# First norm: shift and scale of three tiles summed by TensorE; other orders of splits, exponentials and output blocks in the attentions

## The reference, cut to what matters

```python
mod = (jax.nn.silu(c) @ ada_w[l] + ada_b[l]).reshape(B, 3, 3, 1, D)
n = _modulate(_rmsnorm(h, norm_g[l, 0]), mod[:, 0, 0], mod[:, 0, 1])   # n = norm * (1 + scale) + shift
h = h + 0.5 * mod[:, 0, 2] * _swiglu(n, ffn_w_in[l, 0], ffn_w_out[l, 0])
```

## Time and profile before

| | |
|---|---|
| median of three runs | 3486.48 us |
| profiled execution / its span | 3488.39 / 3486.6 us |
| TensorE busy | 3430.1 us, 98% |
| VectorE busy | 2168.9 us, 62% |
| ScalarE busy | 1322.5 us, 38% |
| GpSimd busy | 296.9 us, 9% |
| mean granted clock of TensorE | 0.997 |

### The profile page before, as it was taken

One profiled execution on the slowest core, in us unless ns is written; L12 is line 12 of the kernel. 1 busy time (PEld: TensorE's weight loads), 2 busy tenths in 40 slices (PEclk: granted clock), 3 DMA queues, 4 the chain that ended last, 5 costly groups with the idle time before them and its releaser, 6 DMA issues.

```text
span 3486.6 us, 46915 instructions
## 1 busy us (share of the span) xinstructions
PE 3430.1 (98%) x18494; PEld 2864.6 (82%) x18494; DVE 2168.9 (62%) x3570; ACT 1322.5 (38%) x1950; POOL 296.9 (9%) x376
## 2 busy tenths in 40 slices
PE   9999999999999999999999999999999999999998
PEld 7888966898888988895789888899988897588888
DVE  7555665656554655566576777788776557655444
ACT  4222463333222422246333523355533236643222
POOL 0000231001000100023100000012100001210000
PEclk9999999999999999999999999999999999999999
DMA  7444302434443344330243344344444312013221
GB/s 277 187 157 163 106 24 100 160 130 172 155 160 148 139 163 159 146 112 3 106 160 137 148 163 154 145 151 176 175 169 163 117 67 90 1 49 112 94 97 49
DMA packets 85561, 452.01 MB, mean 130 GB/s; under 512 B 10304, under 2 KB 12544, under 8 KB 48608
## 3 DMA queue, kind: packets, MB, share of 16 engines
q1 hardware_dynamic: 83168, 439.10, 33.8%
q0 software_dynamic: 2176, 9.92, 0.8%
HBM read 446.88 MB, written 2.10 MB: 129 GB/s over the span
## 4 chain that ended last, share of the span: by engine, by line
PE 89%; DVE 5%; ACT 3%; issue 1%; DMA 0%; POOL 0%; DVEq 0%; SPq 0%; ACTq 0%; POOLq 0%
PE ps L658 22%; PE ps L660 22%; PE ps L659 22%; PE ps L2766 2%; PE ps L2767 2%; PE ps L2768 2%; PE ps L3464 1%; ACT P L1852 1%; PE ps L1035 1%; PE ps L1037 1%; PE ps L1036 1%; PE ps L1772 1%; PE ps L1295 1%; PE ps L1297 1%; PE ps L1296 1%
## 5 line engine op out<-in xcount | busy, mean ns | idle before, releaser
L658 PE MATMUL ps<-nH,WH 128*128 128x512 f32 x2256 | 884.2, 392 | 0.4 <-ACT rot L3195 0.4
L660 PE MATMUL ps<-nH,WL 128*128 128x512 f32 x2256 | 884.2, 392 | 0.0
L659 PE MATMUL ps<-nL,WH 128*128 128x512 f32 x2256 | 883.7, 392 | 0.0
L564 DVE TENSOR_TENSOR WL<-raw,WH 128x2048 fp32r<-128x2048 f32 (+2 forms) x297 | 651.1, 2197 | 370.3 <-ACT WH L553 369.2
L553 ACT ACTIVATE WH<-raw 128x2048 fp32r<-128x2048 f32 (+2 forms) x299 | 543.6, 1823 | 573.5 <-PE ps L660 497.2
L658 PEld LDWEIGHTS ps<-nH,WH 128*128 128x128 f32 x2256 | 423.8, 188 | 95.8 <-issue 3.3
L659 PEld LDWEIGHTS ps<-nL,WH 128*128 128x128 f32 x2256 | 423.8, 188 | 93.0 <-issue 0.2
L660 PEld LDWEIGHTS ps<-nH,WL 128*128 128x128 f32 x2256 | 423.8, 188 | 91.5
L624 DVE SCALAR_TENSOR_TENSOR araw<-araw,cB 128x1024 f32<-128x1024 f32 x224 | 275.6, 1230 | 201.5 <-DMA araw<-in_ast 201.1
L658 PE MATMUL ps<-hH,WH 128*128 128x512 f32 x944 | 372.3, 394 | 1.0 <-DVE h L1262 1.0
L660 PE MATMUL ps<-hH,WL 128*128 128x512 f32 x944 | 371.2, 393 | 0.0
(11 more groups left out here) (451 smaller groups left out, 5910.3 us busy)
## 6 DMA issues: line engine op xcount, KB each, us to landing
raw<-in_wst SPq DMA_DIRECT2D x273, 1024.0 KB, 4.8
araw<-in_ast SPq DMA_DIRECT2D x225, 512.0 KB, 5.7
raw<-in_wst SPq DMA_DIRECT2D x18, 512.0 KB, 3.3
araw<-in_wst SPq DMA_DIRECT2D x9, 1024.0 KB, 4.9
row<-in_ast SPq DMA_DIRECT2D x15, 512.0 KB, 10.6
cw<-in_cw POOLq DMA_DIRECT2D x4, 1024.0 KB, 5.9
h<-in_xT SPq DMA_DIRECT2D x4, 512.0 KB, 5.5
raw<-in_wst SPq DMA_DIRECT2D x8, 256.0 KB, 2.7
```

The lines of the kernel that those rows point to most:

```text
L564: dve.q.tensor_tensor(M.WL[k % NW][:, 0:n], M.raw[raw_use[k]][:, 0:n], M.WH[k % NW][:, 0:n].bitcast(F32), ALU.subtract).then_inc(*v_wlo.up(k))
L658: pe.q.matmul(to, hi[:, i, cc], xh, start=i == 0, stop=False)
L659: pe.q.matmul(to, hi[:, i, cc], xl, start=False, stop=False)
L660: t = pe.q.matmul(to, lo[:, i, cc], xh, start=False, stop=i == nk - 1)
```

## The change

- Shift and scale of tiles 0, 1 and 2 (six rows) are no longer summed by VectorE. The host lays these six 1024x128 matrices with the summed index on the partitions, and `rows(f)` on TensorE does 16 one-column fp32 matmuls for tile f (8 for the shift, 8 for the scale) against silu(c) as a column of 8. `rows(0)` stands ahead of rstd, `rows(1)` and `rows(2)` behind it.
- The fillers of 5 and 14 around rstd are gone, the later one is 8 instead of 14; `part` goes in another order; each engine's work at the start is reordered, and SyncE loads the six matrices first, and the broadcast c behind them.
- Attention 1: ScalarE does the copy between the two exponentials of a step, and VectorE does the lone unit's maximum between the two inverses.
- Attention 2: the split of two weight slots moves from ahead of the units to units 10 and 14 (ScalarE), 11 and 15 (VectorE); a small exponential stands ahead of the units; a fifth output block is begun, behind the last unit.

```diff
--- before.py
+++ after.py
@@ -19,7 +19,7 @@
...
@@ -1402,10 +1414,6 @@
                 t = pe.q.matmul(banks[6][:, j:j + 1], lat.scr[2][:, j * 128:j * 128 + 128], M.ones[:, 0:1], start=True,
                                 stop=True)
             t.then_inc(*mm.up(g, "sum"))
-            warm_up(pe, 5, g, "warm1")
-            pe.wait_ge(*v_dg.to(g))
-            pe.q.matmul(banks[7][:, :], M.ones[:, :], lat.scr[3][:, :], start=True, stop=True).then_inc(*mm.up(g, "rstd"))
-            warm_up(pe, 14, g, "warm2")
             ks = [slot_pe_later("ffn_w_in") for _ in range(3)]
             names = [(g, x, 0, f) for x, f in (("a", 0), ("a", 1), ("b", 0), ("b", 1), ("a", 2), ("a", 3))]
             to = []
@@ -1413,6 +1421,26 @@
                 b, free = take(*name)
                 pe.wait_ge(*free)
                 to.append(b)
+            first_bank[:] = [to[4], to[5], to[4]]
+
+            def rows(f):
+
+                pe.wait_ge(*a_cB.to("first"))
+                if f == 2:
+                    pe.wait_ge(*v_mod.to(g, 0))
+                for m in range(2):
+                    pe.wait_ge(*ld_of(8 * m + f))
+                    w = row_tile(8 * m + f)
+                    for i in range(KT):
+                        t = pe.q.matmul(first_bank[f][:, m:m + 1], w[:, 128 * i:128 * i + 128], M.half[:, i:i + 1],
+                                        start=i == 0, stop=i == KT - 1)
+                t.then_inc(*mm.up(g, "row", f))
+
+            rows(0)
+            pe.wait_ge(*v_dg.to(g))
+            pe.q.matmul(banks[7][:, :], M.ones[:, :], lat.scr[3][:, :], start=True, stop=True).then_inc(*mm.up(g, "rstd"))
+            rows(1)
+            rows(2)
 
             def part(i, which):
                 pe.wait_ge(*a_xhi.to(g, i))
@@ -1431,13 +1459,17 @@
                         if j % 2:
                             mm.again("slot", k)
 
-            part(0, range(4))
-            for i in range(14):
+            part(0, (0, 1))
+            part(1, (0, 1))
+            for i in range(8):
                 pe.q.matmul(banks[6][:, 128:256], M.ones[:, :], M.ones[:, :], start=True, stop=True)
-            part(1, range(4))
-            for i in range(2):
+            part(0, (2, 3))
+            part(1, (2, 3))
+            part(2, range(4))
+            pe.wait_ge(*v_mod.to(g, 2))
+            for i in range(3):
                 part(i, (4, 5))
-            for i in range(2, 8):
+            for i in range(3, 8):
                 part(i, range(6))
...
             g, G, shift = "ffn00", der("ffn00"), mod(1, 0, 0)
             act.q.activation(M.dummy[:, 0:1], M.epsc[:, 0:1], ACT.Silu)
             for i in range(8):
+                if i == 4:
+                    act.wait_ge(*ld_vec.to())
+                    act.q.activation(M.half[:, :], V("c"), ACT.Silu).then_inc(*a_cB.up("first"))
                 act.wait_ge(*h_came(0, 0)(i))
                 if i >= 5:
                     act.wait_ge(*v_ssum.to(g, max(1, i - 5)))
                 act.q.activation(squares_at(i), M.h[:, i, :], ACT.Square).then_inc(*a_sq.up(g, i))
-            act.wait_ge(*ld_cB[0].to("c"))
-            act.q.activation(M.cB[0][:, :], M.cB[0][:, :], ACT.Silu).then_inc(*a_cB.up("c"))
             act.q.activation(M.dummy[:, 1:2], M.epsc[:, 0:1], ACT.Sqrt)
-            now.dummy = 2
+            now.dummy = 3
             act.wait_ge(*mm.to(g, "sum"))
             act.q.activation(lat.rs[:, 0:4], banks[6][:, 0:4], ACT.Sqrt, bias=M.epsc[:, 0:1], scale=1.0 / D
                              ).then_inc(*a_rt.up(g, "sum"))
-            split_act(act, 2)
+            split_act(act, 1)
+            act.q.activation(M.dummy[:, 2:3], M.epsc[:, 0:1], ACT.Silu)
             for i in range(8):
+                if i == 2:
+                    split_act(act, 2)
+                    act.wait_ge(*ld_cB[0].to("c"))
+                    act.q.activation(M.cB[0][:, :], M.cB[0][:, :], ACT.Silu).then_inc(*a_cB.up("c"))
                 act.wait_ge(*v_gain.to(g, i))
                 act.wait_ge(*v_xr.to(g, i))
                 if i >= 2:
@@ -1472,7 +1510,7 @@
                                  bias=shift[:, i:i + 1]).then_inc(*a_ev.up(g, "aff", i))
                 act.q.activation(lat.nH[:, i, :], lat.scr[i % 2][:, :], ACT.Identity, scale=G[:, i:i + 1],
                                  bias=shift[:, i:i + 1]).then_inc(*a_xhi.up(g, i))
-                split_act(act, {1: 3, 5: 4}.get(i, 0))
+                split_act(act, {2: 3, 5: 4}.get(i, 0))
...
-            dve.wait_ge(*v_row.to(8 + f))
-            dve.q.tensor_tensor(two, two, bias, ALU.add).then_inc(*v_mod.up(g, f))
+            if f < NF0:
+                dve.wait_ge(*mm.to(g, "row", f))
+                dve.q.tensor_tensor(two, first_bank[f][:, 0:2], bias, ALU.add).then_inc(*v_mod.up(g, f))
+            else:
+                dve.wait_ge(*v_row.to(8 + f))
+                dve.q.tensor_tensor(two, two, bias, ALU.add).then_inc(*v_mod.up(g, f))
...
                     dve.q.tensor_tensor(ssum, ssum, squares_at(i), ALU.add).then_inc(*v_ssum.up(g, i))
-            start_row_dve(dve, 0)
             dve.wait_ge(*ld_id.to())
...
-            for i in range(8):
-                if i:
-                    start_row_dve(dve, i)
-                if i == 2:
-                    low(1)
-                start_row_dve(dve, 8 + i)
-                if i >= 3:
-                    low(i - 1)
-                start_gain_dve(dve, g, i)
+            def scaled(i):
+
                 if i >= 2:
                     dve.wait_ge(*a_xhi.to(g, i - 2))
                 else:
                     dve.wait_ge(*mm.to(g, "rstd"))
                 dve.q.tensor_tensor(lat.scr[i % 2][:, :], M.h[:, i, :], banks[7][:, :], ALU.mult).then_inc(*v_xr.up(g, i))
-                if i == 0:
-                    split_dve(dve, 1)
-                    low(0)
-                    split_dve(dve, 2)
-                if i == 2:
-                    split_dve(dve, 3)
+
+            for i in range(2):
+                start_gain_dve(dve, g, i)
+                scaled(i)
+            split_dve(dve, 1)
+            low(0)
+            start_gain_dve(dve, g, 2)
+            scaled(2)
+            low(1)
+            split_dve(dve, 2)
+            start_row_dve(dve, 3)
+            low(2)
+            start_row_dve(dve, 11)
+            start_gain_dve(dve, g, 3)
+            scaled(3)
+            split_dve(dve, 3)
+            for i in range(4, 8):
+                if i == 4:
+                    low(3)
+                start_row_dve(dve, i)
+                if i > 4:
+                    low(i - 1)
+                start_row_dve(dve, 8 + i)
+                start_gain_dve(dve, g, i)
+                scaled(i)
             low(7)
             now.rows["dve"] = 16
 
@@ -1833,10 +1886,13 @@
             now.dummy += 1
             act.wait_ge(*v_rope.to(*before))
             for n in range(N1 + FAR):
-                for u in pair_of[n] if n < N1 else ():
+                these = pair_of[n] if n < N1 else ()
+                for u in these[:1]:
                     exp1_act(act, g, u)
                 if NEAR <= n < N1 + NEAR:
                     turned1_act(act, g, pair_of[n - NEAR][0])
+                for u in these[1:]:
+                    exp1_act(act, g, u)
                 if n >= FAR:
                     out1_act(act, g, n - FAR)
 
@@ -1952,9 +2008,14 @@
                 dve.wait_ge(*a_whi.to(k))
                 dve.wait_ge(*v_wlo.to(k))
             for n in range(N1 + FAR + 1):
-                for u in pair_of[n - 1] if 1 <= n <= N1 else ():
+                before, these = pair_of[n - 1] if 1 <= n <= N1 else (), pair_of[n] if n < N1 else ()
+                for u in before[:1]:
                     inverse1_dve(dve, g, u)
-                for u in pair_of[n] if n < N1 else ():
+                if len(these) == 1:
+                    top1_dve(dve, g, these[0])
+                for u in before[1:]:
+                    inverse1_dve(dve, g, u)
+                for u in these if len(these) > 1 else ():
                     top1_dve(dve, g, u)
                 if n == 0:
                     hidden(1)
@@ -3427,7 +3488,7 @@
             output = merge_end_pe()
             for u in range(U2 + 4):
                 if u in (U2, U2 + 1):
-                    output[0](pe, 2 * (u - U2))
+                    output[0](pe, 2 * (u - U2), 2 * (u - U2) + 1)
                 if u < U2:
                     hh, qt = UNITS2[u]
                     pe.wait_ge(*v_hn.to(f"q{hh}"))
@@ -3449,6 +3510,7 @@
                             t = pe.q.transpose(b[:, 128 * x:128 * x + 128], M.Pb[(u - 3) % 4][:, 128 * c:128 * c + 128],
                                                M.ident[:, :])
                         t.then_inc(*mm.up("t2", u - 3, part))
+            output[0](pe, 4)
             return output[1]
 
         def value2_pe(pe, u):
@@ -3486,13 +3548,14 @@
                     turn_head_act(act, name)
                 if n < 2:
```

(43 more changed lines are left out.)

## The result

The changed kernel takes 3497.96 us (median of 7 runs, 3495.11 to 3502.55); in the same rounds the kernel before takes 3487.91 (median of 7 runs, one of which took 12850.38). The ratio is 1.0027, 95% interval 1.0017 to 1.0036: slower, and outside the range predicted (3479.5 to 3495.5). The profiled execution took 3498.03 us with a span of 3496.2.

A forecast was written before the change was run, and what follows sets the result against it. TensorE, 89% of the chain and busy 98% of the span, was taken as the bound. Start 8.7 lost, less 0.9, 2.1 and 1.8 won, gave 3.9 us slower: 3490.4 us on the median, range 3479.5 to 3495.5.

The forecast's parts named there:

- The start: Up to line 658: TensorE's added one-column matmuls at half clock delay the first product; end 70.9 against 62.24, 8.7 us lost.
- the bound on the one-column pace: At the start, one tile's 16 matmuls at half clock take 3.45 us at least, 6.9 at most; 6.9 was taken.
- (a): Rival at the start: rstd alone lifts the clock again for 3.4 us, so 3.4 less, 3487.0; chance 0.18.
- (b): Rival at the start: the clock halves but one-column matmuls keep their pace of 0.108, 3482.4; chance 0.12.
- (c): Rival at the start: the clock never falls, 1.7 us won there, 4.8 with the attentions, 3480.0; chance 0.12.
- Attention 1: Earlier copy and maximum win about 0.6 us per pass, a later exponential loses 0.45; net 0.9 us won.
- rival (d): In attention 1 TensorE waits for the second exponential: 2.7 us lost, with a weaker attention 2 3495.7; chance 0.13.
- the sign of rival (d): In attention 1, more waits for line 1852 than 4 us per layer, listed as showing the forecast wrong.
- Attention 2: Splits and table load moved from ahead of the units: 2.1 us won; fifth output block in a wait: 1.8 won.
- the sum: Whole kernel: the start's loss less the attentions' three gains, 3.9 us slower, 0.11%, within what counts as the same.
- The loads are no limit: At the start, rows 0 and 8 land by 11.8 us, and slot 0 at 14.3, before they are needed.
- my base: The profiled execution of the kernel before, 3488.39 us, 1.9 above the median, to which 3.9 was added.

The follow-up runs named there:

- wide128: The changed kernel with the moving operand of its 48 row matmuls 128 columns wide instead of one; 3489.41 us, ratio 0.9998.
- narrow_filler: The kernel before with its 28 filler ones-products ahead of line 658 one column wide instead of 128; 3491.64 us, ratio 1.0010.
- both_att: The kernel before with the new orders of attention 1 and 2 alone, its start as before; 3485.32 us, ratio 0.9987.
- pad3mb: The kernel before with 3 MB of zeros that nothing reads appended to the weight stream; 3490.68 us, ratio 1.0000.
- after_again: The changed kernel, unedited, run once more beside the kernel before; 3496.84 us, ratio 1.0015.
- wide_even: wide128 with 92 TensorE records taken out of its first ones-products by making them wider; 3485.24 us, ratio 0.9986.

## Why the prediction was wrong

- **The start (8.7 lost): right.** Half clock from 14.4 (measured 14.8, until 38.7: "past 36"), one-column records of 0.215 us in it (13.65 / 64 = 0.213), rstd reached at 17.8 (17.65), the first product at 33.7 (33.01), line 658 at 70.9 (70.48). 8.24 us were lost. The upper end of the bound on the one-column pace, not the lower, was the value.
- **Rivals (a), (b), (c): fallen.** The clock did not rise behind rstd, the records did not keep 0.108, and it did fall. For (c) the rule of the Trainium skill's page "TensorE: Matmul & The Clock Gate", section "Why this matters for your kernels" (keep it busy without gaps), did not hold here: 23.00 of 23.00 us busy at 0.50. What wide128 adds is that the number of columns made the difference in this start; narrow_filler points the same way. That the fall at 2315 is missing in three traces says that the rule "one column doesn't hold the clock" is safe for a long stretch of such records, as here, and not for a short one.
- **Attention 1 (0.9 won): right in sign, too small.** both_att won 0.94 in the first and 0.88 in the second, twice the term. I gave 0.15 us to each of six places, and the wait for the copy did go:

```profile
PE ps L1805 <- ACT P L1908: 4.6, 13, 0.5
PE ps L1786 <- ACT P L1908: 1.1, 3, 0.4
```

  Those two rows are the kernel after from 460 to 560 us. No wait for line 1781's copy is left, and the waits for the exponentials are shorter each (0.5 at most against 0.7) and more of them. They sum to 5.7 us, over the 4 us that the prediction gave as the sign of rival (d); but the kernel before has 4.3 there by the same view, so that sign could not tell the two apart. Which edit gives how much wasn't measured. Rival (d), a loss here, fell.
- **Attention 2 (2.1 and 1.8 won): right.** 2.35 and 1.55 in the changed kernel, 2.31 and 1.54 in both_att. The waits of the earlier trace rows are 0.3 for `Vtk` and 0.2 for the exponentials, and that for `nL` is gone.
- **The step that failed is the sum.** "8.7 - 0.9 - 2.1 - 1.8 = 3.9" takes a shift at the start to pass unchanged through all that follows. Its four terms measured 8.24 - 2.07 - 2.35 - 1.55 = 2.3 in the changed kernel, against 9.6 in the spans. The missing term is +4.6 between 2650 and 2730 us: 92 more TensorE records move the blocks in which its program is fetched, two packets fall on transfers that VectorE waits for at once, both groups land 1.2 to 1.6 us later, TensorE has run out of work after the second and waits 3.0 us, and its clock is half for 3.4 us behind. The text said "The loads are no limit" with the start's loads alone in view. Nothing in it counted instructions.
- **The rest, 2.7 us, is not settled.** In the profiled execution the lag rises by about 1.3 and 1.5 us at the stretches of half clock at 1605.4 and 3138.0, and by 1.2 from 3455 us to the end, and falls by some 1.3 in small steps elsewhere. Steps of this kind need no edit of the instructions: pad3mb runs the program of before, and its trace is 2.4 us longer, with rises near 1500, near 3110 and at the end. They come and go between executions of one kernel (after_again has no fall at 1605), and what sets them off was not tried. I had taken my base as a fixed time: over the later sets the kernel before is at 3490, 3.5 above the three runs I started from, and the changed kernel 6.7 above that, not 10.1. For these 6.7 the runs have start 8.2 (by the traces), orders -4.8 by both_att's times, jump 4.2 by wide128 less wide_even, together 7.6, which agrees within what single medians can tell.

The Trainium skill's page "Runtime: NRT & Kernel Launch", section "Instruction fetch mechanics", says that each engine refills its program in blocks of 16 KB, 256 instructions, through a DMA queue of its own, and that crossing a block costs little and is "mostly hidden". The traces agree on the block. Whether TensorE itself ever waits for its program no row here shows. What the traces add is the cost to a data transfer in flight: 1.2 to 1.6 us on its landing.

## What to carry to other kernels

Count the instructions that an edit adds or removes, not only their time: in a long straight program it moves every later fetch against every transfer, and where an engine waits for a transfer at once, a packet listed with 1 us was some 1.5 us on the landing here. If a gain or a loss shows up far from an edit, look for an instruction packet inside the transfer ahead of it, and try the same edit with its instruction count evened out. Where a long row of products costs its weight loads anyway, try a wide moving operand: in this start the pace stayed nearly the same (0.114 us a record against 0.108), and the clock came back up.

## What the runs showed that I had not expected

- One packet of the instruction queue (16 KB, 0.9 to 1.4 us) inside a group of 2.1 MB of transfers moved the last landing from 7.3-7.6 to 8.5-8.9 us, in every one of the 13 cases where it came before the group's last 0.8 us or so (6.1 us from the issue or earlier).
- A one-column fp32 product in a solid stream paces at 0.108 us a record at full clock and 0.213 at half; with 128 columns at 0.114 at full.
- In a long row, a product's width alone decided whether the clock came back: 96 one-column records ran at half clock for 23.9 us, and at 128 columns the half clock ended after 3.4. In short rows it isn't certain: 28 records of one column were followed by 3.4 us at half clock (one trace), and the 24 near 2312 in 10 traces of 13.
- The same program's runs differ by 3 to 11 us, and profiled executions differ in which of several marginal waits is followed by a stretch of half clock, at about 1.5 us each.
